# A hybrid decoder step: in the output projection, VectorE's weight split is moved behind the two halves of a block

## The reference

```python
def merge_mixers(att, ml_h, mo, p, dtype):
    ...
    ml = (jax.nn.sigmoid(mo + p['b_og']) * ml_h)
    cat = concatenate([rmsnorm(att, p['g_attn_out']), rmsnorm(ml, p['g_mlstm_out'])], axis=-1)
    return cat @ p['w_out']          # 1024 x 1024
...
    h1 = x + merge_mixers(att, ml_h, mo, p, x.dtype)
```

## Time and profile before

| | |
|---|---|
| time, median of three runs | 2257.61 us (2256.64 to 2257.64) |
| the profiled execution: time, and its span from first to last instruction | 2258.22 us, 2256.1 us |
| TensorE matmul, weight load: busy share of the span | 89%, 83% |
| VectorE, ScalarE, GpSimd | 43%, 19%, 4% |
| mean granted TensorE clock over the span | 0.944 |
| the output projection in the span | about 871 to 1014 us |

### The profile page before, as it was taken

How to read it: one execution, slowest core, us unless ns; L and a number is a source line. 1 busy time by engine, 2 the same in 40 slices (tenths; PEclk the granted TensorE clock), 3 DMA queues, 4 the chain that set the end, 5 groups by cost and what they waited for, 6 DMA issues and landing times.

```text
span 2256.1 us, 30064 instructions
## 1 busy us (share of the span) xinstructions
PE 1997.9 (89%) x13010; PEld 1877.3 (83%) x13010; DVE 969.0 (43%) x1668; ACT 432.5 (19%) x805; POOL 91.4 (4%) x89
## 2 busy tenths in 40 slices
PE   5998888998377697868998789899999999999997
PEld 5996658998367456768897569899999999999997
DVE  7223762246565445458224113533333433333344
ACT  2004660001321034003103320300000000000016
POOL 3000002000121020000000000000000000000000
PEclk8999999999688699889999999999999999999999
DMA  4205601110054485103303231111111111111112
GB/s 148 97 28 210 243 21 38 40 44 10 15 205 150 151 374 195 56 28 114 92 19 131 105 110 46 38 41 36 45 56 37 37 48 46 46 35 53 43 38 80
DMA packets 166005, 189.03 MB, mean 84 GB/s; under 512 B 15927, under 2 KB 153687, under 8 KB 161178
## 3 DMA queue, kind: packets, MB, share of 16 engines
q1 hardware_dynamic: 164378, 154.19, 20.9%
q10 hardware_dynamic: 1536, 33.56, 3.9%
HBM read 170.95 MB, written 50.33 MB: 98 GB/s over the span
## 4 chain that ended last, share of the span: by engine, by line
PE 49%; DVE 2%; ACT 2%; issue 1%; DMA 0%; DVEq 0%; ACTq 0%
PE psum L253 43%; PE psum L1960 2%; PE psum L1632 1%; ACT scratch L1653 1%; PE psum L1750 1%; DVE weights_lo L210 0%; DVE scratch L1690 0%; PE psum L1763 0%; DMA weights_raw<-in_w_cv_dram 0%; PE psum L1788 0%; PE psum L1621 0%; ACT wide L1812 0%; DVE weights_hi L208 0%; PE psum L1936 0%; PE psum L1581 0%
## 5 line engine op out<-in xcount | busy, mean ns | idle before, releaser
L253 PE MATMUL psum<-x_hi,weights_hi 128*128 128x384 f32 (+1 forms) x2136 | 483.1, 335 | 56.0 <-DVE x_lo L291 23.5
L253 PE MATMUL psum<-x_lo,weights_hi 128*128 128x384 f32 (+1 forms) x2328 | 521.3, 332 | 0.0
L253 PE MATMUL psum<-x_hi,weights_lo 128*128 128x384 f32 (+1 forms) x2136 | 477.5, 332 | 0.0
L208 DVE CAST weights_hi<-weights_raw 128x1024 fp32r<-128x1024 f32 (+1 forms) x138 | 92.0, 667 | 833.0 <-PE psum L253 819.4
L253 PEld LDWEIGHTS psum<-x_hi,weights_hi 128*128 128x128 f32 x2136 | 371.6, 192 | 63.0 <-issue 51.1
L253 PEld LDWEIGHTS psum<-x_lo,weights_hi 128*128 128x128 f32 x2328 | 405.2, 191 | 0.0
L253 PEld LDWEIGHTS psum<-x_hi,weights_lo 128*128 128x128 f32 x2136 | 371.2, 191 | 0.0
L210 DVE TENSOR_TENSOR weights_lo<-weights_raw,weights_hi 128x1024 fp32r<-128x1024 f32 (+1 forms) x138 | 161.7, 1172 | 4.7
L1876 ACT ACTIVATE scratch<-scratch 128x1088 f32<-128x1088 f32 x22 | 24.5, 1114 | 419.8 <-DVE scratch L1890 419.8
L253 PE MATMUL psum<-hidden_hi,weights_lo 128*128 128x384 f32 (+1 forms) x432 | 95.2, 328 | 0.0
L253 PE MATMUL psum<-hidden_hi,weights_hi 128*128 128x384 f32 (+1 forms) x432 | 95.2, 328 | 0.0
(11 more groups left out here) (341 smaller groups left out, 2423.7 us busy)
## 6 DMA issues: line engine op xcount, KB each, us to landing
weights_raw<-in_w_in_dram SPq DMA_DIRECT2D x28, 512.0 KB, 3.7
work<-in_cache_win_k_dram SPq DMA_DIRECT2D x6, 2048.0 KB, 12.9
work<-in_cache_win_v_dram ACTq DMA_DIRECT2D x6, 2048.0 KB, 13.3
weights_raw<-in_w_gate_dram SPq DMA_DIRECT2D x22, 512.0 KB, 3.8
weights_raw<-in_w_up_dram SPq DMA_DIRECT2D x22, 512.0 KB, 3.7
weights_raw<-in_w_down_dram SPq DMA_DIRECT2D x24, 384.0 KB, 3.4
weights_work<-in_cache_mem_k_dram SPq DMA_DIRECT2D x8, 1024.0 KB, 4.9
work<-in_cache_mem_v_dram SPq DMA_DIRECT2D x8, 1024.0 KB, 11.7
```

The costliest lines, as they stand in the source:

```text
L208: nc.vector.tensor_copy(whi[:, w, 0:nk, :], raw[:, w, 0:nk, :]).then_inc(w_high, 1)
L253: mm = nc.tensor.matmul(PS[:, 3 * s + c, 0:n], w[:, slot, k0 + k], x[part][:, k0 + k, t0:t0 + n], start=(k == 0 and w is whi and part == 0 ...
```

## The change

In the loop over the eight blocks, the split of later weights stood first (for the first block: between the two halves). It now stands behind the attention half's addition, in all blocks in one place. Nothing else is edited: the instructions and their waits are the same.

```diff
             for j in range(KB):
-                split_at(dve, n0 + j + 2 if j + 2 < KB else NB["mk"] + j + 2 - KB) if j else None
                 dve.wait_ge(ml_half_ready, j + 1)
...
                 chain(nc.vector.tensor_tensor(XT[:, j], XT[:, j], out_part[:, 0], ALU.add))
                 if j == 0:
-                    split_at(dve, n0 + 2)
                     dve.wait_ge(rnorm_ready, J["att"][1] + 1)
                 dve.wait_ge(z_ready, n0 + j + 1)
...
                 nc.vector.tensor_tensor(XT[:, j], XT[:, j], out_part[:, 1], ALU.add).then_inc(z_taken, 1)
+                split_at(dve, n0 + j + 2 if j + 2 < KB else NB["mk"] + j + 2 - KB)
                 if j:
                     add_square(dve, nacc, j - 1, N, J["cross"][0])
```

## The result

The changed kernel took 2222.65 us (median of four runs, 2218.02 to 2223.94) against 2257.62 (2256.64 to 2258.76) for the kernel before, run beside it: a ratio of 0.9841, 95% interval 0.9824 to 0.9858. Forecast were 2221.5 us, within 2217 to 2233. The profiled execution has a span of 2221.8 us, 34.3 less than before. Lines behind the edit move up by one or two: the mLSTM pair is now L1519 and L1524, the attention pair L1529 and L1531, the turns of the memory tokens L1558.

What follows compares the result with a forecast made beforehand. Neither engine was taken as the bound: TensorE and VectorE wait for each other once a block. Gains of 22.5 + 10.8 + 2.8 = 36.1 us gave 2221.5 us from the 2257.61 median, range 2217 to 2233.

Steps and rivals of the forecast that it cites:

- the three terms of the sum: Gains in the projection stage: 22.5 us of TensorE holes, 10.8 us of slow rows, 2.8 us at the stage's end.
- the cover of the loads: Slack of weight loads before their split in the eight-block loop: 20 us, with 4.0 us for the landing.
- The idle time: TensorE's six holes between blocks, waiting for VectorE to give back the mLSTM banks, go: 22.5 us gained.
- The margins: In each block, attention banks, mLSTM banks and split weights are ready 3.2, 4.4 and 7.3 us before TensorE asks.
- The clock: Rows behind each hole no longer run slow; granted clock 1.00 instead of 0.87 in the stage: 10.8 us, bounds 0 to 10.8.
- The rival in which the clock does not come back: Holes in the blocks go but rows still run 0.91 us apart as often: 25.3 us gained, 2232.3 us; chance 0.08.
- The first block: The later split of block 2's weights costs 0 in block 1; cover 1.9 us at the attention pair, 6.0 at the split.
- The loads: Weight loads, released by the split two blocks earlier, still land in time in the loop: cost 0.
- The end of the stage: Block 7's mLSTM pair is done before TensorE's last matmul, so the next stage starts sooner: 2.8 us gained.
- The sum: Whole gain in the projection stage: 22.5 + 10.8 + 2.8 = 36.1 us, giving 2221.5 us; chance 0.86.
- What follows the stage: Later stages keep their work but meet the clock's changes at another moment: 0, with 4 us either way.
- the slower rival: Weights landing late at the split hold up the next mLSTM multiplication in VectorE's queue: about 2270 us; chance 0.03.

Runs made afterwards that it cites:

- two extra multiplications: The changed kernel with two needless VectorE multiplications of 1.3 us behind the split in blocks 0 to 6: 2222.42 us, one run.
- the holes filled: The kernel before, with 21 useless matmuls into an unused PSUM bank ahead of TensorE's wait for the mLSTM banks in blocks 2 to 7: 2246.01 us.
- four extra multiplications: The changed kernel with four needless VectorE multiplications of 1.3 us behind the split in blocks 0 to 6: 2232.51 us, one run.
- late weights: The changed kernel, with the weights of block j (2 to 7) sent for only when TensorE has finished block j - 2: 2220.46 us, one run.
- The split between the halves: The changed kernel with the split moved between the mLSTM and attention halves in all eight blocks: 2220.95 us, ratio 0.9839 to the kernel before.
- two early splits: The changed kernel with the square sum ahead of the wait for the block's end and the first two splits ahead of the previous stage's last VectorE copy: 2219.69 us.

## Why the prediction was right

The mechanism and the three terms of the sum are confirmed. Two smaller readings were off: the cover of the loads, and the time behind the stage, which was put at 0.

- *The idle time.* Forecast 22.5 us from six holes; the holes are gone. The clock's term measured by itself leaves, of the 33.34 us that the blocks lost (116.84 − 83.50), 22.6 for them. The margins held: two extra multiplications fitted, four did not.
- *The clock.* Forecast 10.8 us, taken at the upper bound; 10.70 measured with the holes filled. The rival in which the clock does not come back is out: 1.00 over the blocks. One set of banks per half is no cause of pauses here, so long as it is given back in the other half's 6 us. The Trainium skill's rule ("TensorE: Matmul & The Clock Gate", Part 1, "A second HAM failure mode: psum-queue depth-cycling") tells of short idle times between groups of matmuls in a kernel that cycles through PSUM banks; with the change there are none. Where there were some, the traces agree with it for the 3.5 us of the kernel before (0.89) and not for the 0.7 to 1.66 us of the run with four extra multiplications (1.00).
- *The first block.* Forecast at 0. The first split in the loop starts at 890.14 and TensorE goes through block 1 without a hole.
- *The loads.* Forecast at 0, and 19.3 us of delay changed nothing on TensorE. The cover up to the split, forecast at 20 us, was 18.
- *The end of the stage.* Forecast 2.8 us; 2.78 measured, alone and with the change.
- *The sum.* 36.1 forecast, 36.11 in the stretch.
- *What follows the stage.* Taken as 0 with 4 us either way; it was 2.55 us back in the profiled execution, so this is the term that was mis-sized, though inside its allowance. Two runs of matmuls account for it (chain of waits, the change, then the second run before the change):

```profile
983.29 6.88 PE psum L253 x42
...
995.23 8.38 PE psum L253 x48
...
1228.17 5.45 PE psum L1631 x32
```

```profile
1264.57 3.82 PE psum L1632 x32
```

The run of 48 of the earlier trace rows had taken 7.29 us and takes 8.38, at a granted clock of 0.68 instead of 0.80; a run of 32 in the cross attention takes 5.45 us instead of 3.82, at 0.69 instead of 1.00: 1.09 and 1.63 us, a part of which later waits take up. This is more than the chance of one execution. In the four traces with the change's order and its stretch of 91.58 us (the change twice, two extra multiplications, late weights) the first run takes 8.17 to 8.38 us and the second 5.45, and from the first turn to the end of the span it is 1243.8 to 1244.2 us. In the other eight the first takes 7.29 to 7.66, the second 3.8 in six and 5.45 in two, and it is 1241.5 to 1243.1. The split between the halves has the same stretch and the lowest of these (1241.5). So some 2 us that the change gains in the stage are given back behind it, counted against one trace of the kernel before. What sets the moment at which the clock falls there stays open.

That the forecast of 2221.5 us lies 1.2 us from the median is in part luck: beside these 2 us, the first row of block 1 lies anywhere between 884.1 and 888.1 us in the nine traces where nothing ahead of it was edited.

The place at which the prediction was tested least is the slower rival: none of the runs brought a load late enough for it to show.

## What to carry to other kernels

Look at what stands at the head of an in-order queue when its engine idles: an instruction that waits for the other engine's whole block, ahead of one whose input is already there, makes two engines take turns, though each has time to spare. Move the waiting instruction behind what is ready, and check each result that it owes against the moment at which it is asked for. A hole on TensorE costs its length and can cost slow rows behind it (here 3.5 us did, 1.6 did not); a fill of useless matmuls separates the two, and is a cheap test before an order is rewritten. Look behind the stage too: a gain there can be given back in part where later matmuls meet a lower clock.

## What the runs showed of the hardware

Holes of 0.70 to 1.66 us, one in each block, left the granted clock at 1.00 through six blocks, while holes of 3.5 us had brought the mean over the blocks to 0.89 and cost 1.8 us each beyond their length. I had expected a lower clock there as a possibility.

The Trainium skill ("Perfetto Trace Analysis", "Optimization Strategy") says of consistent bubbles, the same gap again and again on the engine that should be full, that they can mean too little SBUF or PSUM for the next tile. Here six like gaps vanished with the same PSUM banks and the same two slots of weights: the order of VectorE's queue was the cause.

A load of 512 KB that landed in 4.0 us in the projection took 8.9 us at the stage's start (its split began 8.97 us behind its issue, in the run with two early splits), where the residual and the cache of the sample were loaded at the same time.
